# Expert weights fetched as whole matrices of 16 KB rows into pairs of places, and one more wait on GpSimd in the mixer

## The reference, cut to what matters

```python
def expert_block(args):
    xb, e = args
    h = jax.nn.silu(xb @ w_gate[e]) * (xb @ w_up[e])
    return h @ w_down[e]
```

## Time and profile before

| | |
|---|---|
| median of 3 runs | 2846.53 us |
| the profiled execution | 2844.54 us, span 2842.7 us |
| mean granted TensorE clock | 0.951 |
| TensorE busy | 2531.6 us, 89% |
| VectorE busy | 1263.4 us, 44% |
| bytes moved by DMA | 703.57 MB, 248 GB/s over the span |
| expert stage, layer 0 | from about 1645 to 2185 us |
| expert stage, layer 1 | from about 2313 us to the end |

### The profile page before, as it was taken

How to read it: one execution, slowest core, us unless ns; L and a number is a source line. 1 busy time by engine, 2 the same in 40 slices (tenths; PEclk the granted TensorE clock), 3 DMA queues, 4 the chain that set the end, 5 groups by cost and what they waited for, 6 DMA issues and landing times.

```text
span 2842.7 us, 37997 instructions
## 1 busy us (share of the span) xinstructions
PE 2531.6 (89%) x16098; PEld 1641.2 (58%) x16098; DVE 1263.4 (44%) x2571; ACT 382.0 (13%) x851; POOL 211.6 (7%) x224
## 2 busy tenths in 40 slices
PE   9999999999999999999999999866667999666665
PEld 5779755896669947699458785322223675222221
DVE  4766644775466656777556543000002553000102
ACT  1410002100131001310022111000000412000000
POOL 0300012000120000400003000000000310000000
PEclk9999999999999999999999999987879999978888
DMA  8354443644535435254431858999999447999998
GB/s 321 119 163 167 175 143 120 193 167 145 192 106 177 178 119 203 93 192 157 157 116 50 292 223 335 421 422 421 421 421 391 183 186 285 421 421 421 421 421 341
DMA packets 245773, 703.57 MB, mean 248 GB/s; under 512 B 18795, under 2 KB 123753, under 8 KB 197219
## 3 DMA queue, kind: packets, MB, share of 16 engines
q1 hardware_dynamic: 244304, 699.30, 65.0%
q10 hardware_dynamic: 1299, 1.83, 0.2%
HBM read 698.20 MB, written 1.05 MB: 246 GB/s over the span
## 4 chain that ended last, share of the span: by engine, by line
PE 73%; DMA 19%; SPq 5%; ACT 2%; DVE 1%; issue 1%; DVEq 0%; ACTq 0%
PE lin L909 46%; PE sco L909 15%; PE trp L909 9%; DMA ring<-in_moe_w_up 6%; SPq L741 4%; DMA ring<-in_moe_w_gate 4%; DMA arena<-in_moe_w_down 3%; DMA ring<-in_moe_w_down 2%; DMA arena<-in_moe_w_gate 2%; PE trp L1078 1%; DMA arena<-in_moe_w_up 1%; PE trp L1174 1%; SPq L746 0%; SPq L743 0%; ACT arena L2328 0%
## 5 line engine op out<-in xcount | busy, mean ns | idle before, releaser
L909 PE MATMUL lin<-ring,arena 128*128 128x512 f32 (+4 forms) x2260 | 771.9, 537 | 15.2 <-DMA ring<-in_moe_w_down 7.3
L909 PEld LDWEIGHTS lin<-ring,arena 128*128 128x128 f32 (+1 forms) x2260 | 367.6, 177 | 337.6 <-issue 313.3
L909 PE MATMUL sco<-ring,arena 128*32 128x512 f32 (+2 forms) x1340 | 330.6, 785 | 161.8 <-DMA ring<-in_moe_w_up 56.9
L909 PE MATMUL lin<-arena 128*128 128x128 f32 (+9 forms) x3312 | 455.4, 348 | 21.6 <-DMA ring<-in_moe_w_down 7.4
L909 PE MATMUL sco<-arena 128*32 128x512 f32 (+6 forms) x1888 | 405.9, 463 | 58.5 <-DMA ring<-in_moe_w_gate 25.4
L3723 DVE TENSOR_TENSOR arena<-arena,sco 128x512 f32<-128x512 f32 x16 | 11.0, 687 | 761.0 <-PE sco L909 761.0
L909 PEld LDWEIGHTS lin<-arena 128*128 128x128 f32 (+4 forms) x3312 | 290.0, 163 | 99.6 <-issue 79.5
L909 PEld LDWEIGHTS sco<-ring,arena 128*32 128x32 f32 (+1 forms) x1340 | 89.1, 147 | 327.4 <-issue 325.2
L909 PEld LDWEIGHTS sco<-arena 128*32 128x32 f32 (+3 forms) x1888 | 158.8, 160 | 156.3 <-issue 148.2
L909 PE MATMUL trp<-arena 128*128 128x128 f32 (+2 forms) x1584 | 217.7, 292 | 1.1 <-ACT arena L2491 0.7
L2780 POOL TENSOR_TENSOR roots<-roots 128x1 f32<-128x1 f32 (+2 forms) x42 | 38.8, 925 | 2283.4 <-DVE roots L2902 2261.0
(11 more groups left out here) (367 smaller groups left out, 2377.8 us busy)
## 6 DMA issues: line engine op xcount, KB each, us to landing
ring<-in_w_gate_up SPq DMA_DIRECT2D x88, 1024.0 KB, 5.9
ring<-in_moe_w_up SPq DMA_DIRECT2D x82, 1024.0 KB, 26.8
ring<-in_moe_w_gate SPq DMA_DIRECT2D x75, 1024.0 KB, 27.0
arena<-in_moe_w_down SPq DMA_DIRECT2D x56, 1024.0 KB, 27.0
ring<-in_moe_w_down SPq DMA_DIRECT2D x51, 1024.0 KB, 26.7
ring<-in_w_down SPq DMA_DIRECT2D x44, 1024.0 KB, 5.2
arena<-in_moe_w_gate SPq DMA_DIRECT2D x44, 1024.0 KB, 26.7
arena<-in_moe_w_up SPq DMA_DIRECT2D x34, 1024.0 KB, 26.9
```

Of the source, the lines that this page charges most:

```text
L909: return nc.tensor.matmul(o, lhsT, rhs, start=start, stop=stop, skip_group_check=not one_group)
```

## The change

1. Where two places lie next to each other, and the piece is not of the last group of eight, the two halves of a matrix go there in one DMA of 2 MB with rows of 16 KB per partition. SP waits for both places first. The landing is counted once, at the first of the two. 82 of layer 0's and 84 of layer 1's matrices are joined; the rest stay in halves.
2. Places are dealt as pairs: (12,13), (14,15), (16,17), ring pairs (0,1) to (10,11), (19,20) in layer 1 as one, and (18,20) in layer 0 and (22,21) always as two single ones. Layer 1 no longer uses 18. Of a group of four pairs the first places take the first halves, the second places the second halves.
3. Features are ordered by eights (gate, up) and fours (down) in place of fours and twos: `moe_x` (L2594), the transposes of the hidden rows (L2010) and the rare overflow path (L761) follow. The number of compute instructions stays.
4. ScalarE's copy of `xa_head_v[1]` in round 0 of layer 0 (L2626) moves behind the eviction of the transposed hidden rows (L2629).
5. In the mixer GpSimd waits for `x_ready` between the first and second operation of `start_inverse`.

In layer 0 SP's order is now, joined ones in brackets: (12,13) (14,15) (10,11) (16,17) gate; (0,1) 18 (2,3) (4,5) 20 up; (6,7) (8,9) 22 (12,13) 21 down; 14, 15, 10, 11 memory; (16,17) (0,1) (2,3) (4,5) gate; ... and in round 7 (2,3) (4,5) (6,7) (8,9) gate; 22 (2,3) (4,5) (6,7) 21 up; 12, 14, 16, 22, 13, 15, 17, 21 down. In layer 1: (12,13) (14,15) (6,7) (8,9) gate; (16,17) (10,11) (19,20) (0,1) up; (2,3) (4,5) 22 (12,13) 21 down; (14,15) (6,7) (8,9) (16,17) gate; ... and in round 7 (0,1) (2,3) (4,5) 22 21 gate, (6,7) (8,9) (10,11) (12,13) up.

```diff
 def expert_slots(first, layer):
...
+    def ring_pairs(first):
+        return [((first + odd + n) % RING, (first + odd + n + 1) % RING) for n in range(0, RING, 2)]
+
+    oldest, behind = ring_pairs(first), ring_pairs(first + count)
+    free = [(RING + n, RING + n + 1) for n in range(0, EXPERT_EXTRA, 2) if RING + n not in SUMS_PLACES]
+    sums, end = [tuple(SUMS_PLACES)], [(COLUMNS_PLACE, X_PLACE)]
+    if ahead:
+        once = free + oldest[0:1] + sums + oldest[1:2] + [(VALUES_PLACE, KEYS_PLACE)] + oldest[2:] + end
+        cycle = free + oldest[0:1] + sums + oldest[1:] + end
     else:
         once = []
+        cycle = free + oldest[0:2] + sums + oldest[2:3] + [(MEMORY_PLACE, KEYS_PLACE)] + oldest[3:] + end
+    rest = count // 2 - len(once)
+    elsewhere = [unit for unit in cycle if unit not in oldest]
+    units = once + cycle * (rest // len(cycle))
+    units += behind[:rest % len(cycle) - len(elsewhere)] + elsewhere
...
+        group = units[m // 2:m // 2 + TOGETHER]
+        places += [a for a, _ in group] + [b for _, b in group]
+        if m + 2 * TOGETHER < count:
+            partner.update({m + i: m + i + TOGETHER for i, (a, b) in enumerate(group) if b == a + 1 and a != VALUES_PLACE})
...
-                def pieces(e, order, down_order=None):
-
-                    for name in ("moe_w_gate_2", "moe_w_up_2"):
-                        for k in range(2):
-                            yield A[name][layer, e, k * 512:(k + 1) * 512, :].rearrange(order, p=P)
-                    for f in range(2):
-                        yield A["moe_w_down_2"][layer, e, f * 256:(f + 1) * 256, :].rearrange(down_order or order, p=P)
+                def pieces(e):
+
+                    for name in ("moe_w_gate_2", "moe_w_up_2", "moe_w_down_2"):
+                        whole = A[name][layer, e, :, :].rearrange("(p k) n -> p k n", p=P)
+                        half = whole.shape[1] // 2
+                        for k in range(2):
+                            yield whole[:, half * k:half * k + half, :], whole
...
+                for m, (src, whole) in enumerate(sources()):
+                    if m in joined:
+                        continue
+                    s = slots[m]
+                    await_place(m)
+                    if m in partner:
+                        await_place(partner[m])
+                        sp.dma_start(two_slots(s), whole.rearrange("p k n -> p (k n)")).then_inc(slot_full[s], 16)
+                        continue
...
-                        s = next(next_slot)
-                        pe.wait_ge(slot_full[s], full[s].next(16))
+                        m, s = next(next_slot)
+                        if m not in joined:
+                            pe.wait_ge(slot_full[s], full[s].next(16))
...
-                    for half in range(2):
-                        every_second = pair_h[:, half * 256:(half + 1) * 256].rearrange("p (f k) -> p k f", k=2)
-                        for f in range(2):
-                            b = 2 * half + f
-                            last = nc.tensor.transpose(trp[:, banks[0], b * P:(b + 1) * P], every_second[:, f, :], ident[:, :])
+                    every_fourth = pair_h.rearrange("p (f k) -> p k f", k=4)
+                    for b in range(4):
+                        last = nc.tensor.transpose(trp[:, banks[0], b * P:(b + 1) * P], every_fourth[:, b, :], ident[:, :])
...
-                    last = nc.scalar.activation(moe_x[:, t, :, :, :], x[:, t, :].rearrange("p (h f k) -> p h k f", h=2, k=4), ACT.Copy)
+                    last = nc.scalar.activation(moe_x[:, t, :, :, :], x[:, t, :].rearrange("p (f h k) -> p h k f", h=2, k=4), ACT.Copy)
...
                 settle(nc.gpsimd.tensor_tensor(rw_XT[:, t, :, :], rw_G[:, t, :, 0, :], mask("rw_levels"), ALU.mult))
+                pool.wait_ge(x_ready, t + 1)
                 nc.gpsimd.tensor_tensor(rw_XT[:, t, :, :], mask("rw_eye"), rw_XT[:, t, :, :], ALU.subtract).then_inc(first_inverse, 1)
```

More of the change, by code:

```diff
@@ L78, in expert_slots @@
 def expert_slots(first, layer):
[L80 to L86, removed]
+    ahead = layer + 1 < SECOND_LAYERS
@@ new lines, in expert_slots @@
+    count = ROUNDS * PIECES + (2 * len(EARLY_MEMORY) if ahead else 0)
+    odd = first % 2
+    def ring_pairs(first):
[6 more added lines that the diff above has]
+        cycle = free + oldest[0:1] + sums + oldest[1:] + end
@@ L87, in expert_slots @@
     else:
         once = []
[L89 to L96, removed]
@@ L97, in expert_slots @@
-    places = once + cycle * (whole // len(cycle)) + last
+        cycle = free + oldest[0:2] + sums + oldest[2:3] + [(MEMORY_PLACE, KEYS_PLACE)] + oldest[3:] + end
[3 more added lines that the diff above has]
+    units += behind[:rest % len(cycle) - len(elsewhere)] + elsewhere
+    assert len(units) == count // 2
+    places, partner, m = [], {}, 0
+    for n in range(0, 4 * (count // 8), 4):
+        if ahead and m == PIECES:
+            for unit in units[m // 2:m // 2 + len(EARLY_MEMORY)]:
+                places += unit
+            m = len(places)
+        if m >= count:
+            break
+        group = units[m // 2:m // 2 + TOGETHER]
+        places += [a for a, _ in group] + [b for _, b in group]
+        if m + 2 * TOGETHER < count:
+            partner.update({m + i: m + i + TOGETHER for i, (a, b) in enumerate(group) if b == a + 1 and a != VALUES_PLACE})
+        m += 2 * TOGETHER
@@ L98, in expert_slots @@
+    assert len(places) == count
     taken, earlier = {}, []
@@ L101, in expert_slots @@
         taken[s] = m
-    for n, s in enumerate(behind):
-        assert taken[s] <= count - RING + n
-    return places, earlier
+    for n in range(RING):
+        assert taken[(first + count + n) % RING] <= count - RING + n
+    return places, earlier, partner, set(partner.values())
 FFN_UNITS = D_FF // (2 * P)
@@ L531, in slot_rows, with two_slots @@
             return ring[:, s, :] if s < RING else extra[:, s - RING, :]
+        def two_slots(s):
+            if s < RING:
+                both = ring[:, s:s + 2, :]
+            elif s < RING + EXPERT_EXTRA:
+                both = extra[:, s - RING:s - RING + 2, :]
+            else:
+                both = spare[:, :, :]
+            return both.rearrange("p a n -> p (a n)")
         def values_ahead(layer):
@@ L712, in sources @@
                     for i in range(ROUNDS):
-                        for part in zip(*[pieces(i * TOGETHER + n, "(p k) n -> p k n") for n in range(TOGETHER)]):
+                        for part in zip(*[pieces(i * TOGETHER + n) for n in range(TOGETHER)]):
                             yield from part
@@ L1903, in moe @@
                 expert_rows = [slice(n * PLACES, (n + 1) * PLACES) for n in range(TOGETHER)]
-                slots, _ = expert_slots(place[0], layer)
+                slots, _, _, joined = expert_slots(place[0], layer)
                 place[0] += len(slots)
-                next_slot = iter(slots)
+                next_slot = iter(enumerate(slots))
                 def early_memory():
@@ L1913, in early_memory @@
                         for _ in range(2):
-                            s = next(next_slot)
+                            _, s = next(next_slot)
                             pe.wait_ge(slot_full[s], full[s].next(16))
@@ L1946, in last_outputs @@
                 def last_outputs():
-                    last_slots = [next(next_slot) for _ in range(TOGETHER)]
+                    last_slots = [next(next_slot)[1] for _ in range(TOGETHER)]
                     for n in range(2):
@@ L2629, in moe @@
                     nc.scalar.activation(pair_hT.rearrange("p a b -> p (a b)"), trp[:, banks[0], :], ACT.Copy).then_inc(tr_done, 1)
+                    if i == 0 and values_ahead(layer):
+                        nc.scalar.activation(xa_head_v[1], lin[:, 0, :].rearrange("p (t n) -> p t n", t=NT), ACT.Copy).then_inc(proj_done, 1)
                     act.wait_ge(tr_full, t_tr.next())
@@ L3716, in moe @@
                     V.tensor_scalar(moe_sum[:, t, :], x[:, t, :], ALPHA_2, None, ALU.mult).then_inc(y_added, 1)
-                slots = expert_slots(place[0], layer)[0]
+                slots, _, _, joined = expert_slots(place[0], layer)
                 for i in range(ROUNDS):
@@ L3734, in moe @@
                 t_selection.skip(1)
-                for s in slots:
-                    if s < RING:
+                for m, s in enumerate(slots):
+                    if s < RING and m not in joined:
                         ring_fill[s] += 16
```

11 lines of the change are left out of this document (4 added, 7 removed).

## The result

The changed kernel takes 2864.61 us (median of 4 runs, 2862.98 to 2864.9); the kernel before took 2846.99 us beside it (4 runs, 2846.32 to 2848.76). The ratio is 1.0057, with a 95% interval from 1.0045 to 1.007: 16 us slower. The profiled execution took 2862.98 us, its span is 2861.2 us, 18.5 more than before.

The account below looks back on a forecast made before the run. TensorE bounds the kernel outside the expert stages, transfers inside them. 6.2 + 9.8 + 8.6 + 2.5 - 10.7 - 2.0 = +14.4 us on the profiled 2844.5 gives 2858.9; with 2.0 for the median, 2861 us, range 2843 to 2872.

Parts of the forecast that it names:

- Rows: Expert weight transfers: 16 KB rows save 0.075 us per joined matrix, for 143 outside the starts, -10.7 us.
- the second rival: Expert stages: whole per-packet cost goes (21.4 us), TensorE keeps its clock; -1.8 us in sum, 2845; chance 0.18.
- the third rival: Expert weight transfers: a 16 KB row moves as two 8 KB packets, nothing gained; +25.1, 2871.6 us; chance 0.10.
- Layer 0's start: Layer 0's first expert round: (12,13) asked for only at 1744.9, others behind it; 26th MB lands later, 6.2 us lost.
- Layer 1's start: Layer 1's first expert round: (12,13) asked for only at 2407.4; four MB short of before, 9.8 us lost.
- Layer 0's last round: Between gate and up: pairs free only when both halves are read, so the queue empties; 8.6 us lost.
- Last halves of up: Both layers: up's two halves start together after its last landing and end later; 2.5 us lost.
- Mixer: GpSimd's wait frees VectorE's L3481 for tiles 0 and 1, TensorE's half clock may go: -2 us (0 to -3.5).
- the queue is deep enough: Expert stages: places coming 5 or 8 us later starve nothing, only gains stay; 2834 us; chance 0.12.

Follow-up runs that it names:

- the clean run: The fastest kernel (0.996) with its 137 joined matrices issued as two 1 MB transfers in 8 KB rows, each asking for its own place: 2846.5 us, ratio 0.9998.
- the order alone: Changed kernel with no matrix joined; new order of places and features and the mixer's wait stay, 1 MB pieces ask singly: 2859.61 us, ratio 1.004.
- the run that undoes it: Changed kernel with gate and up of layer 0's last round not joined, each place asked for when its own half is read: 2853.49 us, ratio 1.0022.
- the best version: Changed kernel, layers' first and layer 0's last rounds in single pieces, pair places consecutive; layer 1 regains place 18, 22 before 5: 2834.14 us, ratio 0.996.

## Why the prediction was right, and where it was not

Slower was right, and 2864.6 lies in the range, 3.6 above the number. By the changes of one part at a time, the 16 us are: the wait -3.4, the order of places +14.8 (0.9988 to 1.004), asking by pairs +12.5 (to 1.0084), long rows -7.7 (to 1.0057). Each has an uncertainty of some 4 to 5 us by the ratios; the stage times, one execution each, say 14.7, 10.5 and -7.0 for the last three. The series is one way through the edits, and its steps are not shares of the changed kernel's own loss: the 14.8 are what single pieces lose in the new places, by waits for 8 and 12 that the pairs don't have; the pairs lose as much at the starts by waits of theirs.

Term by term, from the two profiled executions (predicted, then measured):

- **Rows**, -10.7, measured -11.5: layer 0 made up 6.0 between its 30th and 180th MB, layer 1 5.5 from its 30th to its last (against pairs of 8 KB rows, where nothing but the rows differs, 5.2 and 5.1 in the same stretches). The price of 0.075 per joined matrix was 0.079 in the clean run. The continuation of two rates (410, 421) to 427 or 428 held; the second rival's full saving of the packets did not, nor did the third rival's two packets per row. (For that rival the text said that no row was longer than 8 KB. The trace of before did have packets of 16384 bytes, 129 of them, all instruction loads and none of a weight.) The estimate worked out above from the 425 GB/s of the Trainium skill, "DMA: Bandwidth & Descriptors", section Bandwidth, would have been too small: 0.024 per MB, where 0.039 was measured.
- **Layer 0's start**, +6.2, measured +8.4. **Layer 1's start**, +9.8, measured +11.6. Sizes right to 2.2 us each, and the path to them is that of the trace: the pair (12,13) is asked for 100.2 and 93.9 us after the stage's first issue, which is the predicted point in both layers, what stood behind it in SP's order waited with it, and the queue had run dry some 2 us before. What fell is what this seemed to say about the cure. Single pieces in the same places gain only 1.9 and 1.1, and the order alone, with single pieces, loses 6.8 and 9.5 without the pair. The text knew one way to starve this queue, a place that is free late, and the kernel has a second: free places behind one that is not. No run takes apart (12,13) alone, so how much of the 8.4 and 11.6 that pair makes by itself, and how much the ring pairs ahead of it ((4,5) in layer 1, see the window from 2404), is not shown. The rest of the miss is in part the time that the queue takes after a dry stretch: (12,13) lands 8.5 and 7.7 us after its issue (1743.7 to 1752.2, 2419.5 to 2427.2), where I had put 7.2. That is 1.3 of 2.2 us in layer 0 and 0.5 of 1.8 in layer 1; for the remainder no run gives a cause.
- **Layer 0's last round**, +8.6, measured +10.0 up to the 188th MB, and 10 by the run that undoes it. Here the reason holds as given, the half clock included. Two things were sized too low: the time from gate's landing to the issue of (2,3), 9.8 us where I had 8.8 (TensorE's halves took 9.6, not 8.7), and from there to the landing, 7.8 where I had 7.2. The long rows of the four matrices take 0.3 off.
- **Last halves of up**, +2.5, measured +0.35 at the end of layer 1 (0 to 1.3 in the seven profiles of kernels with long rows there: 15.3 to 16.6 us from the last landing to the end, where all five with 8 KB rows have 15.3). TensorE waits for the last column half of layer 0 as long as before (0.74 us against 0.73), so its cover was enough there. But the halves' lateness came back by another way that the text hadn't: place 22, refilled for down, waits for up's first half until 2174.0 in place of standing in the queue, and lands 0.8 us late.
- **Mixer**, -2, measured -1.2 in the two profiles, 1.6 in the mean of all profiles, 3 by the ratios. Both runs of L3518 near 0.68 came as said. The full clock behind them came too, 2.08 us for 64 products in place of 3.63, but no run shows it as an effect of the wait, since the changed kernel without the wait has it as well.

That the total is closer than its parts is luck: the misses are 6.2 us upwards and 2.15 downwards, and leave 4. Together +2.2, +1.8, +1.4, -1.35 (0.8 and 0.35 in place of 2.5), -0.8 for the rows and +0.8 for the mixer, on the sum of 14.4: 18.45, the spans' difference.

The rival "the queue is deep enough" fell in every place that it needed. In the thick, where the text costed nothing for asking late, the run of pairs with 8 KB rows agrees: 30th to 180th MB of layer 0 in 374.4 us, against 374.3 with single pieces.

What stays open: the share of the pair (12,13) by itself, as said above, and where the last 1.6 us of layer 0's start stay in the best version. 22, which stands behind 9 there, would be the first thing to move; no run did it. In layer 1 hardly anything is left: at the 31st MB the best version is 0.2 us behind the kernel before.

## What to carry to other kernels

A longer row pays a small sum on every byte, and a place asked for late costs a whole gap: here 0.04 us per MB against 8 to 12 us per gap. So join transfers where the queue is deep, and keep single pieces where it is shallow, in the first round of a stage and where a place is reused at once. When you take a transfer apart, look at the order of its halves again. Here that turned +0.57% into -0.18%, and place 18 with the exchange beside it made it -0.40%, of which the mixer's wait is some 0.12. And when a queue issues in program order, write beside each place the time at which it comes free; a place that stands behind one that is free later can be a loss of its own, whatever the size of the transfers, if the queue is dry by then.

## What the runs showed that was not expected

- The order of places, with the same bytes, rows and count of transfers, costs 14.8 us (1.004 against 0.9988), some 2.5 of it for place 18, which that order does without; 10.5 us with the same places in both (1.0049 against 1.0012).
- Joining halves takes away the head start of the first half. At the one place where TensorE's start gates the queue, this cost 3.5 us (29.9 against 26.4 for eight MB).
- TensorE's granted clock can differ between two profiles in one stretch of the same code: the same 64 products of the mixer took 3.63 us in the profile of before, at 0.50, and 2.08 in that of the kernel without the wait, whose mixer is the same code, at 1.00. The window of the latter, beside the last of the earlier trace rows:

```profile
1522.00:1524.00 2.00, 1.46 (x50) 1.46 (x52) 2.00 (x4) 0.27 (x1) 2.00 (x2) 1.00 0.00 0
```

  A single profile of each kernel would have credited the wait with 1.5 us that the other kernel without it doesn't lose.
